# A two-block network on one core: x loaded from ScalarE's queue, and the four MoBA heads of a mixing stage computed two at a time

## The reference, cut to what matters

```python
h = rms_norm(x, norm_mix_g[l]); p = h @ w_in[l]
y_a = conformer_conv(...)                    # 31-tap depthwise conv, layer norm, silu
y_b = moba_attention(q, k, v)                # 4 heads of 64; 256 tokens are one block: plain causal softmax
y_b = head_rms_norm(y_b, moba_out_g[l], 4)
y_c = gla_chunked(q_c, k_c, v_c, log_a)      # 4 heads, state of 64x128 carried over 8 chunks of 32
y_c = head_rms_norm(y_c, gla_out_g[l], 4) * silu(r)
x = x + concatenate([y_a, y_b, y_c]) @ w_out[l]
```

## Time and profile before

| | us |
|---|---|
| three runs | 1286.14, 1285.66, 1282.18; median 1285.66 |
| the profiled execution | 1284.62 |
| its span, first to last instruction | 1282.9 |
| outside the span | 1.7 |

### The profile page before, as it was taken

One profiled execution on the slowest core, in us unless ns is written; L12 is line 12 of the kernel. 1 busy time (PEld: TensorE's weight loads), 2 busy tenths in 40 slices (PEclk: granted clock), 3 DMA queues, 4 the chain that ended last, 5 costly groups with the idle time before them and its releaser, 6 DMA issues.

```text
span 1282.9 us, 16669 instructions
## 1 busy us (share of the span) xinstructions
PE 1254.9 (98%) x6276; PEld 1030.8 (80%) x6276; DVE 821.7 (64%) x954; ACT 673.4 (52%) x806; POOL 147.1 (11%) x168
## 2 busy tenths in 40 slices
PE   7999999999999999999999999999999999999998
PEld 5888888888898678888887778888888877888886
DVE  5466455545567655555459876877746987677763
ACT  6554264434356554444356455676526554776652
POOL 2000000000010000000029510000004931000000
PEclk9999999999999999999999999999999999999999
DMA  8544554446364236445543425544562423544540
GB/s 324 226 164 180 181 197 178 171 179 227 131 246 165 86 121 237 181 168 224 198 138 132 136 94 197 197 160 167 192 226 103 171 103 131 194 168 165 195 180 33
DMA packets 32534, 220.13 MB, mean 172 GB/s; under 512 B 4000, under 2 KB 4032, under 8 KB 6752
## 3 DMA queue, kind: packets, MB, share of 16 engines
q1 hardware_dynamic: 30384, 213.40, 45.1%
q0 software_dynamic: 1664, 5.41, 1.3%
q10 hardware_dynamic: 432, 0.57, 0.1%
HBM read 218.31 MB, written 1.05 MB: 171 GB/s over the span
## 4 chain that ended last, share of the span: by engine, by line
PE 92%; DVE 5%; ACT 1%; issue 1%; POOL 1%; DMA 0%; POOLq 0%; ACTq 0%
PE acc L1516 27%; PE acc L1518 26%; PE acc L1517 26%; PE tb L1548 5%; DVE wlo L953 2%; PE acc L1703 1%; PE acc L1705 1%; PE acc L1706 1%; DVE cacc L1282 1%; PE tb L1910 1%; ACT whi L494 1%; PE tb L1617 1%; PE tb L1738 1%; PE tb L1936 0%; PE tb L1757 0%
## 5 line engine op out<-in xcount | busy, mean ns | idle before, releaser
L953 DVE TENSOR_TENSOR wlo<-raw,whi 128x2048 fp32r<-128x2048 f32 x200 | 458.2, 2310 | 235.1 <-ACT whi L494 235.1
L494 ACT ACTIVATE whi<-raw 128x2048 fp32r<-128x2048 f32 x200 | 377.0, 1908 | 109.2 <-PE acc L1518 100.9
L1516 PE MATMUL acc<-whi,xth 128*128 128x512 f32 (+1 forms) x1056 | 418.9, 397 | 7.2 <-DVE wlo L1002 3.0
L1518 PE MATMUL acc<-whi,xtl 128*128 128x512 f32 (+1 forms) x1056 | 409.3, 388 | 0.0
L1517 PE MATMUL acc<-wlo,xth 128*128 128x512 f32 (+1 forms) x1056 | 408.4, 387 | 0.0
L1516 PEld LDWEIGHTS acc<-whi,xth 128*128 128x128 f32 x1056 | 198.6, 188 | 54.0 <-issue 6.3
L1518 PEld LDWEIGHTS acc<-whi,xtl 128*128 128x128 f32 x1056 | 198.6, 188 | 41.3
L1517 PEld LDWEIGHTS acc<-wlo,xth 128*128 128x128 f32 x1056 | 199.0, 188 | 37.0
L1516 PE MATMUL acc<-whi,yth 128*128 128x512 f32 x512 | 204.3, 399 | 1.7 <-DVE ytl L1430 1.7
L1518 PE MATMUL acc<-whi,ytl 128*128 128x512 f32 x512 | 200.4, 391 | 0.0
L1517 PE MATMUL acc<-wlo,yth 128*128 128x512 f32 x512 | 200.3, 391 | 0.0
(11 more groups left out here) (239 smaller groups left out, 1060.5 us busy)
## 6 DMA issues: line engine op xcount, KB each, us to landing
raw<-in_stream SPq DMA_DIRECT2D x200, 1024.0 KB, 4.8
rb<-in_rel_rows POOLq DMA_DIRECT2D x8, 256.0 KB, 2.9
raw<-in_stream SPq DMA_DIRECT2D x4, 256.0 KB, 5.2
raw<-in_stream SPq DMA_DIRECT2D x2, 512.0 KB, 7.0
gs_sb<-in_gs_row POOLq DMA_DIRECT2D x1, 1024.0 KB, 5.5
frow<-in_fin_row POOLq DMA_DIRECT2D x2, 512.0 KB, 5.0
x<-in_x_in SPq DMA_DIRECT2D x2, 256.0 KB, 4.2
x<-in_x_in SPq DMA_DIRECT2D x1, 512.0 KB, 8.2
```

The costliest lines, as they stand in the source:

```text
L494: act.activation(whi[:, s, :], raw[:, s, :], ACT.Copy).then_inc(hi_ready, 1)
L953: dve.tensor_tensor(wlo[:, s, :], raw[:, s, :], whi[:, s, :], ALU.subtract).then_inc(lo_ready, 1)
L1516: pe.matmul(o, xh, wh, start=first, stop=False)
L1518: return pe.matmul(o, xl, wh, start=False, stop=last)
```

## The change

Start: the three loads of x move from SP's queue to ACT's (with the column gains, `gcol`, second among them), so SP issues weight quarters only. Both splits of quarters 2 and 3 of unit 0 come earlier than those of the second half of x. PE turns the second half of x after slice 0 instead of 1 and the second tokens after slice 3 instead of 5.

Mixing stages: the head-by-head functions go. `moba_scores(p)` computes two heads p in four matmuls that alternate between the heads (rows 0 to 63 and 64 to 127, banks `tb[1]` and `tb[2]`); `moba_begin` and `moba_exp` handle both heads, `moba_turn` transposes six tiles, `moba_pv` leaves the unnormalised outputs of all heads in `tb[0]`. The division by the sum and the head norm become one factor: ACT squares `tb[0]` (new), DVE sums, adds epsilon times the squared sum, POOL takes the power -0.5, one DVE multiplication writes `mo`. `gla_out` writes into the accumulator banks of the step before (`pair_bank(4 + pair, b)`). Gating, gain and split of the first tokens (`gated(0)`, `y_gain(0)`, `y_lo(0)`) come ahead of those of the second in DVE's order, `lo(U0+11)` and `lo(U0+12)` come later, and `y_turn(0)`, `mo_turn` and the heads move to earlier places in PE's order.

```diff
 SP
-            sp.dma_start(x[:, 0, 0:512], x_in[0:P, 0:512]).then_inc(x_first, 16)
-            first_part(0, 0)
-            first_part(0, 1)
-            sp.dma_start(x[:, 0, 512:D], x_in[0:P, 512:D]).then_inc(x_loaded[0], 16)
-            for u, i in ((0, 2), (0, 3), (1, 0), (1, 1)):
+            for u, i in ((0, 0), (0, 1), (0, 2), (0, 3), (1, 0), (1, 1)):
                 first_part(u, i)
-            sp.dma_start(x[:, 1, :], x_in[P:2 * P, :]).then_inc(x_loaded[1], 16)
 ACT
+            act.dma_start(x[:, 0, 0:512], x_in[0:P, 0:512]).then_inc(x_first, 16)
             act.dma_start(gcol[:, :, :], cols).then_inc(gains_loaded, 16)
+            act.dma_start(x[:, 0, 512:D], x_in[0:P, 512:D]).then_inc(x_loaded[0], 16)
+            act.dma_start(x[:, 1, :], x_in[P:2 * P, :]).then_inc(x_loaded[1], 16)
...
+                moba_exp(0)
                 o_keep(0)
-                h_keep(0)
-                hi(U0 + 12)
+                moba_exp(1)
+                o_keep(1)
+                moba_keep(0)
                 act.wait_ge(x_btr, l + 1)
...
                 keep(5, rs, 512, ACT.Silu, (0,))
-                h_exp(1)
+                moba_keep(1)
+                hi(U0 + 12)
+                act.wait_ge(s_o, b0 + 2)
+                act.activation(msq[:, :], tb[0], ACT.Square).then_inc(t_sq, 1)
                 keep(5, rs, 512, ACT.Silu, (1,))
-                h_keep(1)
-                h_exp(2)
...
+                hi(U0 + 13)
+                act.wait_ge(t_g, l + 1)
+                act.activation(yth[:, 512:1024], xg[:, 0, :], ACT.Copy).then_inc(t_hi, 1)
                 hi(U0 + 14)
 DVE
...
                 dve.wait_ge(x_or, l + 1)
+                gated(0)
+                lo(U0 + 12)
+                y_gain(0)
+                den = stat[:, 240:248]
+                dve.wait_ge(s_p, 4 * b0 + 8)
+                dve.scalar_tensor_tensor(stat[:, 248:256], den, EPS, den, ALU.mult, ALU.mult).then_inc(t_d2, 1)
+                dve.wait_ge(t_sq, l + 1)
+                dve.tensor_reduce(stat[:, 256:264], msq[:, :].rearrange("p (c d) -> p c d", d=DH), AX.X,
+                                  ALU.add).then_inc(t_ms, 1)
...
+                gated(1)
+                y_lo(0)
+                y_gain(1)
+                dve.wait_ge(t_r, l + 1)
+                dve.tensor_tensor(mo..., tb[0]..., stat[:, 120:128]..., ALU.mult).then_inc(t_y, 1)
+                y_lo(1)
                 lo(U0 + 13)
...
                 lo(U0 + 14)
                 lo(U0 + 15)
 PE
-                             {1: second_half, 5: second_tokens} if j == m == 0 else {}, quarters=j == m == 0)
+                             {0: second_half, 3: second_tokens} if j == m == 0 else {}, quarters=j == m == 0)
...
+                    for m in range(M):
+                        for h in range(2):
+                            r = slice(DH * h, DH * h + DH)
+                            mm = pe.matmul(tb[1 + h][:, P * m:P * (2 * m + 1)], mqT[r, p, P * m:P * m + P],
+                                           mkT[r, p, 0:P * (m + 1)], start=True, stop=True)
...
-                step(5, m0={1: lambda: state_inc(5), 3: all_of((state_inc, (6,)), (first_scores, ())),
-                            5: all_of((ln_turn, ()), (gla_out, (0,)))},
-                     end=lambda: h_t(0),
-                     m1={1: all_of((gla_out, (1,)), (ln_back, ())), 5: all_of((first_pv, ()), (second_scores, ()))})
-                h_s(2)
+                step(5, m0={1: lambda: state_inc(5), 3: all_of((state_inc, (6,)), (moba_scores, (0,))),
+                            5: all_of((ln_turn, ()), (gla_out, (0,)), (moba_scores, (1,))),
+                            7: all_of((gla_out, (1,)), (moba_turn, (0,)))},
+                     m1={1: ln_back, 3: all_of((moba_pv, (0,)), (moba_turn, (1,))), 6: lambda: moba_pv(1), 7: lambda: y_turn(0)})
...
-                        pe.wait_ge(x_yl, 4 * l + (1, 2, 3, 4)[j])
+                    elif j == 3:
+                        pe.wait_ge(t_lo, l + 1)
+                    else:
+                        pe.wait_ge(x_yl, 3 * l + (1, 3, 3)[j])
...
-                    (0, 0): lambda: h_t(1), (0, 1): all_of((h_v, (1,)), (y_turn, (0,))), (0, 2): lambda: y_turn(1),
-                    (0, 3): all_of((h_s, (3,)), (h_t, (2,))), (1, 0): lambda: h_v(2),
-                    (1, 1): all_of((pe.wait_ge, (x_yl, 4 * l + 3)), (h_t, (3,))), (1, 2): lambda: h_v(3),
-                    (2, 2): mo_turn})
+                    (0, 2): lambda: y_turn(1), (1, 2): mo_turn})
```

More of the change, by code:

```diff
@@ L671, in y_hi @@
                 act.activation(yth3[:, 8 + p, :], tb[3][:, SEQ:2 * SEQ], ACT.Copy).then_inc(w_hi, 1)
-            def heads(h0, n, sb, pt, s0, banks):
-                def keep(i):
-                    h = h0 + i
-                    act.wait_ge(t_pt, h + 1)
-                    if i >= 2:
-                        act.wait_ge(t_o, h - 1)
-                    act.activation(pt[:, i % 2, :], banks[i % 2][:, 0:384], ACT.Copy).then_inc(t_ptc, 1)
-                def exp(i):
-                    h = h0 + i
-                    for m in range(M):
-                        act.wait_ge(t_mx, 2 * h + m + 1)
-                        w = sb[:, i % 2, 0:P] if m == 0 else sb[:, i % 2, P:3 * P]
-                        act.activation(w, w, ACT.Exp, bias=stat[:, s0 + 2 * i + m:s0 + 2 * i + m + 1],
-                                       accum_out=stat[:, s0 + 2 * n + 2 * i + m:s0 + 2 * n + 2 * i + m + 1]
-                                       ).then_inc(t_p, 1)
-                return exp, keep
             act.wait_ge(n_r, STATS[2] + 1)
@@ L1395, in _, with y_gain @@
                     last.then_inc(x_on2, 1)
-                finish(1)
-                for m in range(M):
-                    dve.wait_ge(x_ytr, 3 * l + 1 + m)
+                def y_gain(m):
+                    dve.wait_ge(x_ytr, 2 * l + 1 + m)
                     dve.tensor_tensor(xg[:, 1 + m, :].rearrange("p (k t) -> p k t", t=P),
-                                      tb[0][:, :].rearrange("p (k t) -> p k t", t=P),
+                                      tb[1 if m else 3].rearrange("p (k t) -> p k t", t=P),
@@ L1429, in _ @@
[L1429 to L1430 removed]
+                dve.wait_ge(x_or, l + 1)
+                gated(0)
[5 more added lines that the diff above has]
+                dve.wait_ge(t_sq, l + 1)
@@ L1929, in gla_out @@
                         pe.wait_ge(x_St, (NCH - 1) * (l + 1))
-                    else:
-                        pe.wait_ge(x_oc, 2 * l + 1)
+                        pe.wait_ge(x_ev, 10 * l + 8)
+                    o = pair_bank(4 + pair, b)
                     p = slice(DK * b, DK * b + DK)
@@ L1967, in y_turn, with moba_scores @@
                     pe.wait_ge(x_on2, 2 * l + m + 1)
-                    if m:
-                        pe.wait_ge(x_yg, 3 * l + 1)
                     for i in range(4):
-                        mm = turn(tb[0][:, i * P:(i + 1) * P], og[:, m, i * P:(i + 1) * P])
+                        mm = turn(tb[1 if m else 3][:, i * P:(i + 1) * P], og[:, m, i * P:(i + 1) * P])
                     mm.then_inc(x_ytr, 1)
+                b0 = HEADS // 2 + 2 * l
+                def moba_scores(p):
+                    if p:
+                        pe.wait_ge(s_sb, b0 + p)
+                    else:
+                        pe.wait_ge(x_mcp, 2 * l + 2)
+                    for m in range(M):
+                        for h in range(2):
+                            r = slice(DH * h, DH * h + DH)
+                            mm = pe.matmul(tb[1 + h][:, P * m:P * (2 * m + 1)], mqT[r, p, P * m:P * m + P],
+                                           mkT[r, p, 0:P * (m + 1)], start=True, stop=True)
+                    mm.then_inc(s_s, 1)
@@ new lines, in moba_turn @@
+                def moba_turn(p):
+                    pe.wait_ge(s_p, 4 * (b0 + p) + 4)
+                    if p:
+                        pe.wait_ge(s_ptc, 2 * (b0 + p))
+                    else:
+                        pe.wait_ge(s_sb, b0 + 2)
+                    for i in range(6):
+                        o = tb[1][:, P * i:P * i + P] if i < 4 else tb[2][:, P * (i - 4):P * (i - 3)]
+                        mm = turn(o, pp2[p][:, i // 3, P * (i % 3):P * (i % 3) + P])
+                        if i in (3, 5):
+                            mm.then_inc(s_pt, 1)
@@ new lines, in moba_pv @@
+                def moba_pv(p):
+                    pe.wait_ge(s_ptc, 2 * (b0 + p) + 2)
+                    for h in range(2):
+                        pt, c = 3 * P * h, DH * (2 * p + h)
+                        v = [mv[:, kk, c:c + DH] for kk in range(M)]
+                        pe.matmul(tb[0][:, c:c + DH], pt2[:, pt:pt + P], v[0], start=True, stop=True,
+                                  skip_group_check=True)
+                        pe.matmul(tb[0][:, 256 + c:256 + c + DH], pt2[:, pt + P:pt + 2 * P], v[0], start=True, stop=False,
+                                  skip_group_check=True)
```

(3 more changed lines are left out.)

226 lines of the change are left out of this document (85 added, 141 removed).

## The result

| | us |
|---|---|
| kernel before, median of 4 | 1285.26 (1282.18 to 1286.14) |
| changed kernel, median of 4 | 1271.49 (1270.34 to 1272.80) |
| ratio | 0.9896, 95% interval 0.9883 to 0.9908 |
| its profiled execution | 1270.38, span 1268.7 |

The change makes the kernel 1.0% faster. The profiled executions differ by 14.2 us.

What follows compares the result with a forecast made beforehand. The prediction took PE, busy for 98% of the span, to bound the kernel. From 1284.6 us it took 9.2 for both mixing stages (4.6 a layer) and 3.4 for the start: 1272.0 us, range 1268.0 to 1277.5.

Steps and rivals of the forecast that it cites:

- PE's own work: Mixing stages: scores in pairs save 1.64 us and fewer excursions 0.6, sum 2.2 us a layer; bounds 0.6 and 2.6.
- The excursions: Mixing stage: PE's departures from regular matmuls fall from 17 to 11, each costing some 0.1 us, upper price 0.17.
- The waits: Mixing stage: PE's three old waits, for mo, its low part and the norm's first addition, go: 3.3 us a layer.
- The new one: Product's second unit: PE waits for both token tiles at once, 0.9 us a layer with its restart; bounds 0.5 and 2.
- The first addition: Norm at the end of the mixing stage: done at 767.0, wanted by PE at 767.3, so 0.3 us of cover.
- the copy ahead of the v products: Last projection: ACT's copy is ready 1.4 us ahead of the second v product, the smallest cover there.
- The start: Kernel start: second pair of units begins at 22.0 instead of 25.5, taken as 3.4 us; bounds 0 and 4.3.
- x's first half 0.5 us later than now: Start: x's first load shares the way with quarter 0 and lands 0.5 us later, so first matmul at 7.5.
- a first matmul later than 8.5: Start: named beforehand as a sign that the prediction is wrong; 7.5 was laid out.
- The rival that the start pays nothing: Start: bytes limit the first microseconds and x's first half lands later, so no gain there, 1275.4 us; chance 0.18.
- The third rival: Attention, 444 to 460: the clock doesn't fall in a run, saving 3.3 us more, 1268.7 us; chance 0.14.
- Slower: Mixing stages: a late new wait of x = 5 us brings the clock down, further 3.3 us, 1288.6 us; chance 0.03.

Runs made afterwards that it cites:

- e9: Changed kernel with the second head's score matmuls one slice later, behind three regular matmuls: 1276.62 us, 0.9938 of the kernel before.
- e5: Changed kernel with all score matmuls of one head before those of the other: 1272.66 us, 0.9894 of the kernel before.
- e7: Changed kernel with the transposes of y_b and the order of splits behind them put back as before: 1275.43 us, 0.9922 of the kernel before.
- e6: Changed kernel with the product's second unit waiting for the first tokens alone, for the second ones only ahead of their quarters: 1270.91 us, 0.9885 of the kernel before.
- e10: Changed kernel with six extra copies on ACT ahead of its copy of the second pair's transposed scores: 1278.87 us, 0.9951 of the kernel before.
- e4: Changed kernel with x's first half back on SP's queue ahead of the weight quarters: 1270.90 us, 0.9892 of the kernel before.
- e3: Kernel before with only the start's new order of splits and transposes, all loads on SP: 1280.48 us, 0.9965 of the kernel before.

## Why the prediction was right

The median of 1271.49 lies 0.5 us under the forecast of 1272.0. Term by term:

- **PE's own work**, 2.2 us a layer: 2.74 less busy, of which 0.32 are the restarts of two waits (3 before, 1 after), so 2.4. The size and the main cause (1.64 from scores in pairs) hold by e9. The excursions were miscounted: the trace of the kernel before has 16 from the state increment on, not 17, so five went. The 0.8 us that is left of the 2.4 makes 0.15 for each of them, near the upper price of 0.17 rather than the 0.1 that was taken. That the heads must alternate, as I had read out of the earlier trace rows, is refuted by e5; it didn't enter the sum.
- **The waits**, 3.3 less 0.9: idle fell by 1.91 and restarts by 0.32, together 2.2 for 2.4. All three old ones went, two of them by the earlier turn (e7). The new one stands where it was put, at the second unit of the product (746.87), 0.87 and a restart of 0.2 for the predicted 0.9; e6 confirms its whole size, 1.06.
- **Covers.** The first addition was to be ready 0.3 us early and is; the copy ahead of the v products 1.4 us early and is 1.2 to 1.4 (e10). The loads and powers that I costed at nothing have no wait in the list.
- Together 4.6 a layer was forecast and 4.65 measured.
- **The start**, 3.4 us, is the term that was mis-sized: 2.2. The step that failed is "x's first half 0.5 us later than now": it was 1.4 later. I had given quarter 0 a share of the way, but two loads issued at the same moment were both slow. Why they were is argued, not shown (see e4). With x's first half on SP (e4) the rest of the layout nearly holds: the first matmul comes at 7.53 and the second pair at 22.45, where 7.5 and 22.0 had been laid out. The prediction named a first matmul later than 8.5 as a sign of being wrong, and it came at 8.54 (8.45 to 8.85 in the eight traces with this start): on this part the prediction was wrong, and the change of issuer that it counted on cost time. Moreover 2.2 is the favourable value; in half of these traces it is 1.6, because the matmuls come to their 0.23 us later. The rival that the start pays nothing had the right mechanism, a later x, but weighed it too high, since the orders' gain of 3.0 is larger.
- **The clock.** The third rival happened as well, in half of the executions. It was worth 2.7 us, not 3.3, mainly since 0.9 us of the low clock fell into the idle, where it costs nothing (that leaves 2.9). In the profiled execution, 1270.38, it makes good the 1.2 missing at the start: 1272.0 + 1.2 - 2.7 = 1270.5. In the median it counts by about half. So the closeness of 0.5 us is partly luck: two opposite errors of 1.2 and some 1.4 us, and one of them, the clock, differs from execution to execution.
- **Slower**: the mechanism exists, an idle that brings the clock down, and e10 shows that it can set in at a shorter wait than the prediction took for it: 1.37 us in the mixing stage with 1.7 us of clock, instead of 2.94 with 3.3. Behind the kernel's own wait of 0.87 it did not happen in any trace, but neither did it behind the old waits of 1.32 to 1.34. As an estimate, with 1.7 in place of 3.3 it would still take a wait of about 5 us to eat the gain of 13.8 (2 x (5 + 1.7) = 13.4).

What stays open: why the profiled executions of one kernel repeat their clock in the attention while others vary, whether the change shifts how often the clock falls there, and about 1 us between the 11.5 us that the traces assign to the change and the 12.4 to 12.8 of the executions at like clock.

## What to carry to other kernels

Lay the timeline out anew with the durations of the rows, engine by engine, before believing a reordering: the layout gave the place and size of a wait that didn't exist yet. Moving loads to a second issuer made the very load that everything waits for 1.4 us later here, and all of the start's gain came from the order of the work (e3). So try the order first, and keep the opening load ahead of the others. And when a wait names several inputs at once, ask which of them the next matmuls really need: splitting it was worth 1.06 us a layer here.

## What the runs showed of the hardware that I had not expected

- Two groups of fp32 matmuls on 64 rows each, on different row halves, overlap even if all of one come before all of the other in the program (0.86 us for both in e5; 0.84 for one alone in e9).
- Behind an idle of 1.37 us the granted clock was 0.66 from 744 to 748 us (e10, in both layers 3.3 us longer); behind idles of 1.32 to 1.34 and of 1.65 us in other places it stayed at 1.00. The length of the idle alone doesn't decide.
- The first matmuls of 512 columns started 0.43 us apart and later ones 0.23; in the same start this changed at 11.65 us or only behind 13.39, which moved the second pair of units by 0.6 us, with a clock column of 1.00 throughout.
- Two loads of 256 KB issued at the same moment by two engines landed after 4.3 and 4.2 us; with the second issued 0.45 us behind the first on one queue, the first took 2.9 and 3.2. Whether the moment or the queue counts was not separated.
- The same program has executions 2 us apart that differ in the mean granted clock, 0.997 or 0.998 for 0.999 or 1.0.
